# Down products of four feed-forward blocks: high and low activations as one 512-column moving operand

## The reference

```python
def swiglu(h, w_gate, w_up, w_down):
    return (jax.nn.silu(h @ w_gate) * (h @ w_up)) @ w_down
...
x = x + swiglu(h, ffn_w_gate[i], ffn_w_up[i], ffn_w_down[i])      # first stack
...
x = x + g2 * _swiglu(h, ffn_gate[l], ffn_up[l], ffn_down[l])      # second stack
```

## Time and profile before

| | |
|---|---|
| median of three executions | 1247.48 us (1245.53 to 1249.95) |
| the profiled execution's own time | 1249.51 us |
| its span, first to last instruction | 1248.2 us |
| granted TensorE clock, mean over the span | 0.988 |
| PE, PEld, DVE, ACT, POOL busy | 95%, 91%, 74%, 53%, 6% of the span |
| packets of DMA queue q1 (raw and ada loads among them) | 250.36 MB |

### The profile page before, as it was taken

The page is one execution under the profiler, slowest core; times in us unless marked ns, Lnnn a source line. Parts: engine busy times, 40 slices in busy tenths (PEclk is TensorE's granted clock), DMA queues, the critical chain, the costliest instruction groups (busy, mean ns, idle before and its releaser), DMA issues.

```text
span 1248.2 us, 24814 instructions
## 1 busy us (share of the span) xinstructions
PE 1186.6 (95%) x9914; PEld 1130.0 (91%) x9914; DVE 926.3 (74%) x1761; ACT 657.7 (53%) x1143; POOL 80.1 (6%) x91
## 2 busy tenths in 40 slices
PE   7898999999998999999997889999999899999999
PEld 7777999999987999999986779999998778999999
DVE  6646798878777888788788768888885565766653
ACT  6336654445445644446455776544445776544441
POOL 2010000001000100002100011000000222000000
PEclk9999999999999999999999999999999999999999
DMA  7862697878753588778744335887776432666561
GB/s 269 239 178 70 229 311 257 265 264 289 262 190 118 179 268 252 251 239 287 261 135 125 111 113 196 276 255 249 254 289 210 140 111 85 218 182 182 181 201 68
DMA packets 81270, 257.78 MB, mean 207 GB/s; under 512 B 9016, under 2 KB 22020, under 8 KB 81156
## 3 DMA queue, kind: packets, MB, share of 16 engines
q1 hardware_dynamic: 75396, 250.36, 60.9%
q10 hardware_dynamic: 5760, 5.83, 1.9%
HBM read 253.49 MB, written 2.67 MB: 205 GB/s over the span
## 4 chain that ended last, share of the span: by engine, by line
PE 79%; DVE 8%; ACT 4%; issue 3%; DMA 1%; POOL 1%; ACTq 0%; DVEq 0%; POOLq 0%
PE ps L528 71%; PE ps L579 2%; DVE wlo L1274 2%; PE ps L638 1%; PE ps L646 1%; PE ps L637 1%; PE ps L642 1%; DMA UR<-uscr 1%; DVE X L1280 1%; ACT whi L865 1%; DVE aacc L1280 1%; ACT oS L865 1%; ACT HH L865 1%; DVE HL L1280 1%; PE ps L560 1%
## 5 line engine op out<-in xcount | busy, mean ns | idle before, releaser
L528 PE MATMUL ps<-HH,whi 128*128 128x256 f32 (+1 forms) x2152 | 619.7, 288 | 17.8 <-DVE wlo L1274 8.2
L528 PE MATMUL ps<-HL,whi 128*128 128x256 f32 (+1 forms) x2152 | 611.4, 284 | 0.0
L528 PE MATMUL ps<-HH,wlo 128*128 128x256 f32 (+1 forms) x2152 | 610.7, 284 | 0.0
L865 ACT ACTIVATE whi<-raw 128x1024 fp32r<-128x1024 f32 (+1 forms) x364 | 382.3, 1054 | 340.5 <-PE ps L528 325.7
L1274 DVE TENSOR_TENSOR wlo<-raw,whi 128x1024 fp32r<-128x1024 f32 (+1 forms) x364 | 441.8, 1221 | 45.7 <-ACT whi L865 45.3
L528 PEld LDWEIGHTS ps<-HH,whi 128*128 128x128 f32 x2152 | 411.8, 191 | 34.9 <-issue 24.7
L528 PEld LDWEIGHTS ps<-HH,wlo 128*128 128x128 f32 x2152 | 412.6, 192 | 0.0
L528 PEld LDWEIGHTS ps<-HL,whi 128*128 128x128 f32 x2152 | 411.4, 191 | 0.4
L528 PE MATMUL ps<-GH,whi 128*128 128x256 f32 x704 | 195.6, 278 | 0.6 <-DVE bcol L1499 0.5
L528 PE MATMUL ps<-GL,whi 128*128 128x256 f32 x704 | 195.0, 277 | 0.0
L528 PE MATMUL ps<-GH,wlo 128*128 128x256 f32 x704 | 195.0, 277 | 0.0
(11 more groups left out here) (220 smaller groups left out, 937.9 us busy)
## 6 DMA issues: line engine op xcount, KB each, us to landing
raw<-wall SPq DMA_DIRECT2D x363, 512.0 KB, 4.3
araw<-ada SPq DMA_DIRECT2D x96, 512.0 KB, 4.7
UR<-uscr ACTq DMA_DIRECT2D x32, 142.0 KB, 3.8
oBB<-kbias SPq DMA_DIRECT2D x16, 192.0 KB, 2.5
aTB<-scratch SPq DMA_DIRECT2D x12, 128.0 KB
uscr<-U ACTq DMA_DIRECT2D x8, 143.5 KB, 4.9
out<-X SPq DMA_DIRECT2D x8, 128.0 KB, 2.9
aTB<-scratch SPq DMA_DIRECT2D x12, 64.0 KB
```

The lines of the kernel that those rows point to most:

```text
L528: ins = pe.e.matmul(o, l, r, start=(kt == p.order[0] and i == 0), stop=(kt == p.order[-1] and i == 2))
L865: ac.then_inc(ac.e.activation(o, i, func, **kw), sem)
```

## The change

High and low gated activations are put side by side in one tensor GB, 22 rows of 2 x 256 values, high first. GH and GL become views of it; every row starts at a partition address that is 64 bytes beyond a multiple of 128, as the rows of GH and GL did. For the first seven tiles of each down product PE multiplies whi with the whole row of GB, 512 columns, into the whole bank, and wlo with the high half, into the bank's first half. The bank's second half so holds whi times low. VectorE adds it to X in an operation of its own, settles, and then adds the first half as before. The eighth tile of each down product keeps its three matmuls and its one addition.

```diff
-            GH, GL = sb("GH", [P, KF, T], F32R, st), sb("GL", [P, KF, T], F32R, st)
+            GB = sb("GB", [P, KF, 2, T], F32R, st)
+            GH, GL = GB[:, :, 0, :], GB[:, :, 1, :]
...
+        def halves(name, nt):
+
+            return PROD[name].kts == KF and nt < PROD[name].tiles - 1
...
+                        elif halves(name, nt):
+
+                            pe.e.matmul(ps[:, :].rearrange("p (a t) -> p a t", a=2), wh, GB[:, kt, :, :],
+                                        start=(kt == p.order[0]), stop=False)
+                            ins = pe.e.matmul(ps[:, 0:T], wl, hh[:, kt, :], start=False, stop=(kt == p.order[-1]))
+                            mm = []
...
+                    if halves(name, nt):
+
+                        stt(X[:, nt, :], ps[:, T:2 * T], scale(nt), X[:, nt, :], op, ALU.add, S.xlow)
+                        dv.settle()
                     stt(X[:, nt, :], ps[:, 0:T], scale(nt), X[:, nt, :], op, ALU.add, S.ev)
```

More of the change, by code:

```diff
@@ L346, in __init__ @@
         self.hi0, self.lo0 = new("hi0"), new("lo0")
-        self.hh, self.hl = new("hh"), new("hl")
+        self.hh, self.hl, self.xlow = new("hh"), new("hl"), new("xlow")
         self.sq, self.sqa, self.tot = new("sq"), new("sqa"), new("tot")
```

## The result

The changed kernel takes 1251.99 us in the median of twelve executions, the kernel before 1247.56 us beside it; the ratio is 1.0046, with a 95% interval of 1.0024 to 1.0069. A second comparison gave 1.0061 (1.0037 to 1.0084). It is slower by about half a per cent, where 1240.8 us was forecast.

What follows compares the result with a forecast made beforehand. PE was taken to bound the kernel. Savings of 8.2 us from the profiled 1249.5 gave 1241.3, or 7.0 without a slow stretch 1240.5; 1240.8 us was predicted, range 1237.5 to 1247.

Steps and rivals of the forecast that it cites:

- What bounds the kernel: Whole kernel: PE paces it, busy 95% of the span; work elsewhere counts only where PE waits.
- The 512-column matmul: Down stages, whi times the whole GB row: 0.2155 us a step, taken from the plain fp32 record.
- The upper bound, 0.2267: Down stages, wide matmul: at most two of today's 256-column steps, if 0.0067 us belonged to every 256 columns.
- What is in the 0.1134: Down stages, 256-column step: 0.1067 us of columns plus 0.0067 of weight load that the matmul is too short to cover.
- The 256-column matmul with wlo: Down stages, short matmul: keeps 0.1134 us because the next whi loads under it; bounds 0.1087 and 0.118.
- the forecast gain of 7.0: Down stages without a slow stretch: all 616 changed blocks save 0.0113 us each, 7.0 us, giving 1240.5.
- VectorE and the ends of stages: Down stages: 28 added DVE operations, 0.46 us each, hidden by the ring of split weights; waits at stage ends stay.
- The forecast for the loads: Weight loads in the down stages: PE frees units 3% sooner, dn1 draws 297 GB/s; costs nothing, up to 1 us.
- C: Down stages: surcharge belongs to the columns, or two instructions go out; wide matmul 0.2267 us, time 1247.7; chance 0.14.
- B: Down stages: the slow pace, 0.118 us for the short matmul, spreads; gain 5.9 us, time 1243.6; chance 0.17.
- D: Down stages: only a fixed cost per instruction goes, 0.002 us, 1.2 us in all, time 1246.3; chance 0.09.
- E: dn0 to dn2: VectorE becomes the bound; at 1.8 us an added step 13.4 us lost, time 1254.7; chance 0.06.

Runs made afterwards that it cites:

- second half: The changed kernel with VectorE's two additions and its layout, but three 256-column matmuls per block instead of the wide one; 0.9985 of the kernel before.
- layout: The kernel before with only GH and GL made views of one tensor, rows interleaved; 0.9985 of the kernel before.
- HH rows: The kernel before with rows of HH and HL 1152 instead of 1088 bytes apart, starting 64 bytes beyond a multiple of 128; 1.0019 of the kernel before.

## Why the prediction was wrong, point by point

*What bounds the kernel* stands: PE without a gap to speak of in the down stages, at full clock, in both kernels. The HH products kept their pace, as forecast: the mean step in gu0 is 118.3 ns before and after, in gu2 119.8.

*The 512-column matmul* is the step that failed, the term 0.2155. I took it from the plain fp32 record of the earlier trace rows as "the same number of streamed columns per weight load". But that record takes two column times for each of its 256 columns, and an fp32r matmul one for each of its 512; fp32r pays a surcharge with its columns that plain fp32 and bf16 don't. The upper bound, 0.2267, was still too low: measured 0.235, 0.459 ns a column, as in the slow pace. At 0.235 instead of 0.2155 a block is 0.0195 us dearer, 12.0 us over 616 blocks.

*What is in the 0.1134.* The half clock of the earlier trace rows was read rightly as one column a cycle, and wrongly as proof that the columns cost nothing extra at full clock: at 1.2 GHz a column comes every 0.83 ns, longer than the 0.46 that it takes at most, so a limit on the columns can't show there. The weight load only looked like the bound. The 0.11 from its start to the matmul that uses it is the step of the matmuls themselves; its own record lasts 0.19. With a quarter of the weights the step didn't fall.

*The 256-column matmul with wlo* was put at 0.1134, with 0.118 as a bound, and took 0.118: in no trace did a short one beside a wide one have the fast pace (0.117 at best), and in dn0, dn1 and dn3 of the changed kernel even the last tile, three of 256, kept 0.118. That term adds 616 x 0.0048 = 3.0 us, and the last tiles 3 x 66 x 0.0047 = 0.9. 12.0 + 3.0 + 0.9 less the forecast gain of 7.0 gives 8.9 us slower than a kernel with all stages at the fast pace. The traces bear it out: from first to last start the four stages of the changed kernel take 251.1 us, those of the second half 242.2. Measured are 0.46% and 0.61%, 5.7 and 7.6 us. The kernel before isn't at its fast pace throughout: dn2 of its trace is 1.7 us longer than that of the second half. Of the 16 down stages in four traces with three matmuls at place 64 (before, second half, layout, HH rows) 4 ran slow, 1.7 to 2.3 us each, some 2 us a trace. That the unprofiled executions lose as much is an estimate.

*VectorE and the ends of stages* were right: 0.45 us a tile, hidden; the kernel with the second half has all of it, at 0.9985. The forecast for the loads, that freeing units sooner costs nothing, wasn't tested, as no unit was freed sooner.

*Rivals.* C was nearest (the surcharge belongs to the columns) and had 0.14; its time was too good by the step from 0.227 to 0.235 and by the short one's 0.118, and the surcharge isn't in proportion. B had the short one right. D and E are refuted, D by the 0.235, E by the experiment that has all of VectorE's added work. The slower side held only E, the wrong mechanism; C with the slow pace of the earlier trace rows would have given it (this is said with the result known): 0.236 + 0.118, no block shorter than 0.354, which costs every stage that ran fast 2.1 us.

## What to carry to other kernels

Before merging matmuls to save weight loads, find out whether the weight load costs anything: load fewer columns of weights in one stage and see whether the step falls. The price of an instruction is read from one of the same type: the plain fp32 record looks like two passes of the new one, and its 0.2155 was 0.02 us too low. Where an instruction has two paces in one trace, price the new one by the slow pace as well.

## What the runs showed of the hardware

- At full granted clock a 512-column fp32r matmul stepped by 0.228 to 0.236 us, a bf16 one by 0.216; for 256 columns 0.1133 to 0.120 against 0.109. With 32 instead of 128 weight columns the 512-column step stayed at 0.231 to 0.232.
- At half granted clock the surcharge is gone: 0.213 us for 256 columns, and 0.267 for 320 and 0.427 for 512 in the run with other widths.
- Three matmuls of 256 fp32r columns at the same place have two paces, 0.1133 and 0.118 us, which a stage kept until PE paused (dn2 in the earlier trace rows) and which differ between stages and between kernels. What sets them is open.
- The start of the rows, modulo 128 bytes, moves the step of the 512-column matmul by up to 7 ns: 0.235 at 64, 0.228 at 32. For 256 columns at 0 it was 0.120.
- fp32r matmuls of 192 columns, each with its own 128 weight columns, stepped by 0.109 to 0.114 us at full and by 0.213 at half granted clock, like those of 256.
